# A gather-bound decoder layer: searches lead their rounds by one instead of two, and the Scalar engine's copies go ahead of the pairs' steps

## Chip, cores, metric

One core of one Trainium2 chip runs the whole program. The metric is the device time of one execution in microseconds (us), the median of several; the program is otherwise fixed, with float32 inputs and outputs. Engines are named as in the profile: PE (TensorE; PEld is its weight load), DVE (VectorE), ACT (ScalarE), POOL (GpSimd, which issues the gathers) and SP (SyncE, plain loads and stores).

## The reference

One decoder layer for 1024 prompt rows and 8 sample rows of width 1024. A first part (conditioning, normalisation, one projection into a short convolution and a chunked gating, an output projection) is not touched. The second part is a lookup among 16384 experts, each one row of `expert_u` and one of `expert_v`:

```
def peer_block(xb, w_q, sub_keys, expert_u, expert_v):
    q = (xb @ w_q).reshape(tb, 8, 2, 128)                 # 8 heads
    s = einsum('thpc,hpkc->thpk', q, sub_keys)            # 2 x 128 scores
    sv, si = top_k(s, 16)
    cand = sv[:, :, 0, :, None] + sv[:, :, 1, None, :]
    cv, ci = top_k(cand.reshape(tb, 8, 256), 16)          # 16 of the 256 sums
    expert = si[.., ci // 16] * 128 + si[.., ci % 16]     # 8 x 16 = 128 experts per row
    g = softmax(cv)
    act = gelu(einsum('tkd,td->tk', expert_u[expert], xb))
    return einsum('tk,tkd->td', g * act, expert_v[expert])
```

So every prompt row reads 128 rows of `expert_u` and 128 of `expert_v`, 4 KB each: 2048 gathers of 128 rows, 0.5 MB a gather.

## The kernel before, in words

`peer` holds the second part. Its 8 blocks of 128 rows are done in 32 rounds (`ROUNDS`), four to a block; a round is one pair of heads, 32 experts for each of 128 rows (`WIDE = 32`). Each engine has its own program, written out in order, and the engines meet at semaphores only; an engine never passes a waiting instruction.

Round n on each engine:

- POOL issues 32 gathers of `expert_u` for round n, into a ring of 8 row buffers, and between them 32 gathers of `expert_v` for round n-1, into another ring of 8 (L1093, L1105). Gather g of u waits until DVE has done product g-8, a gather of v until PE has used that slot four tiles at a time (`v_used`). The first u gather of a round waits for the round's indices (`u_idx_ready`).
- DVE does the 32 products of a round (`product`, L1350: u row times x row, summed into `dot`), and between them, at products numbered in `places`, one `search` for each head in `heads_of(n)`. A search (`retrieve`, L1268 to L1321) is the two-stage top 16 and ends in `expert_f`. After the odd head of a pair, `soften` (L1332 to L1338) lowers the sums by their maximum, waits for ACT's exponential and divides by the total. The round ends in `weigh` (L1358).
- PE turns the weights of round n-1 (L1464), turns the pair found in round n-1 (`turn_picked`, L1453), and then does 8 quads of round n-1's v rows (`quad`, L1483). After quads 0, 1 and 2 it puts one head each of `heads_of(n)`: `queries` (L1426), `turn_queries` (L1434, waits for ACT's copy `q_sb`), `scores` (L1442, waits for ACT's copy `qT_sb`).
- ACT does the gelu of the dots (L1193), `keep_weight` (L1202), `keep_picked` (L1183), and then for each head of the round `keep_head`: the copies `q_sb` (L1154), `qT_sb` (L1156), `s_sb` (L1160; this one also waits until the search before has read the old scores). After the odd head of a pair comes `picked`: it waits for the end of that head's search, copies the indices `u_idx` (L1169), loads the table of Exp and takes the exponential (L1171), and loads the table of Gelu again (L1172).

Which heads a round holds sets the lead. Before, heads 0 to 3 are projected ahead of round 0 (0 and 1 are searched ahead of it, 2 and 3 within it), and round n takes heads 2n+4 and 2n+5, so a pair is found two rounds ahead of its gathers. From round 20 on a round takes three heads (`places` 6, 14, 22 instead of 10, 19) until all 72 are done: rounds 20 to 28 have three, round 29 one. Of three heads the odd one is second in rounds 20, 22, 24, 26 and 28, and first and third in the others.

```
            for n in range(ROUNDS + 1):            # ACT
                ...
                if n < ROUNDS:
                    for hd in heads_of(n):
                        keep_head(hd)
                        if hd % 2:
                            picked(hd // 2)
```

Of the kernel before, what the change touches and what calls it, by code (L numbers as in the profile page):

```python
# [9 lines left out]
ALU = mybir.AluOpType  # L10
ACT = mybir.ActivationFunctionType
# [3 lines left out]
P = 128  # L15
# [10 lines left out]
TOPK = 16  # L26
# [849 lines left out]
def peer(nc, t, scratch, ident, w_q, spare, keysT):  # L876
# [12 lines left out]
    KEPT = 8  # L889
    LAST = TILES * (ROUNDS - 1)  # L890
    with ExitStack() as ctx:
        def sb(name, shape, dt=F32):
            return ctx.enter_context(nc.sbuf_tensor(name, shape, dt))

        def sem(name):
            return ctx.enter_context(nc.semaphore(name))
# [26 lines left out]
        best = sb("best", [P, 2, TOPK])  # L923
        gate = [sb(f"gate{i}", [P, 2, TOPK]) for i in range(KEPT + 1)]
# [17 lines left out]
        eps = sb("p_eps", [P, 1])  # L942
        warm = sb("warm", [P, 1])
# [27 lines left out]
        def found_in(n):  # L971

            if n < 0:
                return (0, 1)
            return [hd // 2 for hd in heads_of(n) if hd % 2]

        def heads_of(n):


            first = 2 * n + 4 + max(0, n - 20)  # L980
            return range(min(first, HEADS * (NB + 1)), min(first + (2 if n < 20 else 3), HEADS * (NB + 1)))

        def v_place(g):
# [26 lines left out]
        s_done = sem("s_done")  # L1010
        s_copied = sem("s_copied")
        head_step = sem("head_step")
        soft_step = sem("soft_step")
        exp_done = sem("exp_done")
        picked_turned = sem("picked_turned")
# [114 lines left out]
        def _(act):  # L1130
# [5 lines left out]
            def turn(blk):  # L1136

                for n, ps in enumerate((ps_a, ps_b)):
                    act.wait_ge(h2_turned, 2 * blk + n + 1)
                    nc.scalar.activation(h2T[:, 4 * n:4 * n + 4, :], ps[:, :, :], ACT.Copy).then_inc(h2T_done, 1)  # L1140

            def keep_x(blk):

                act.wait_ge(h2_landed, 16 * blk + 16)
                if blk:
                    act.wait_ge(dots_done, WIDE * 4 * blk)
                nc.scalar.activation(ps_x[:, :], h2_in[:, :], ACT.Copy).then_inc(x_kept, 1)

            def keep_head(hd):

                if hd % HEADS == 0 and hd:
                    turn(hd // HEADS)
                act.wait_ge(q_done, hd + 1)
                nc.scalar.activation(q_sb[:, :], flat_a[:, 0:QCOLS], ACT.Copy).then_inc(q_copied, 1)  # L1154
                act.wait_ge(qT_done, hd + 1)
                nc.scalar.activation(qT_sb[:, :], flat_b[:, 0:QCOLS], ACT.Copy).then_inc(qT_copied, 1)  # L1156
                act.wait_ge(s_done, hd + 1)
                if hd:
                    act.wait_ge(head_step, CHAIN * (hd - 1) + SEARCHED)
                nc.scalar.activation(s_sb[:, :, :].rearrange("p a b -> p (a b)"), flat_a[:, 0:QCOLS], ACT.Copy  # L1160
                                     ).then_inc(s_copied, 1)

            def picked(n):

                if n < ROUNDS:
                    act.wait_ge(head_step, CHAIN * 2 * (n + 1))
                    if n >= KEPT:
                        act.wait_ge(dots_done, WIDE * (n - KEPT + 1))
                    nc.scalar.activation(u_idx[n % KEPT][:, :], expert_f[n % 2][:, 0, :], ACT.Copy).then_inc(u_idx_ready, 1)  # L1169
                act.wait_ge(soft_step, 4 * n + 1)  # L1170
                nc.scalar.activation(gate[n % (KEPT + 1)][:, :, :], gate[n % (KEPT + 1)][:, :, :], ACT.Exp).then_inc(exp_done, 1)  # L1171
                nc.scalar.activation(warm[:, :], eps[:, :], ACT.Gelu)  # L1172

            def keep_picked(n):

# [12 lines left out]
            def gelu(n):  # L1188

                act.wait_ge(dots_done, WIDE * (n + 1))  # L1190
                if n:
                    act.wait_ge(weight_done, n)
                nc.scalar.activation(act_u[:, :], dot[:, n % 2, :], ACT.Gelu).then_inc(gelu_done, 1)  # L1193

            def keep_weight(n):

                act.wait_ge(weight_turned, n + 1)
                if n >= 2:
                    act.wait_ge(v_used, QUADS * (n - 1))
                for a in range(4):  # L1200
                    src = ps_weight[32 * a:32 * a + 32, a:P:4].rearrange("p (j r) -> p j r", j=4)
                    last = nc.scalar.activation(diagonal(spread[n % 2], 4, QUADS, a), src, ACT.Copy)  # L1202
                last.then_inc(spread_done, 1)

            def normalise(ps, b, rows):

                if b:
                    act.wait_ge(out_stored, 16 * b)
                act.wait_ge(y_done, b + 1)
                nc.scalar.activation(out_rows[rows, :], ps[rows, :], ACT.Copy).then_inc(y_kept, 1)  # L1210
                act.wait_ge(y_kept, b + 1)
                nc.scalar.activation(y_junk[rows, :], out_rows[rows, :], ACT.Square, accum_out=y_stat[rows, 0:1]
                                     ).then_inc(y_ssq, 1)
                act.wait_ge(y_ssq, b + 1)
                nc.scalar.activation(y_stat[rows, 1:2], y_stat[rows, 0:1], ACT.Sqrt, scale=1.0 / D, bias=eps[rows, 0:1]
                                     ).then_inc(y_std, 1)

            keep_x(0)
            turn(0)
            for hd in range(4):  # L1220
                keep_head(hd)
                if hd % 2:
                    picked(hd // 2)
            for n in range(ROUNDS + 1):
                if n >= 1:
                    gelu(n - 1)
                if n % 4 == 0 and 4 <= n < ROUNDS:
                    keep_x(n // 4)
                if n % 4 == 1 and n >= 5:
                    normalise(ps_y, n // 4 - 1, slice(0, P))  # L1230
                if n >= 1:
                    keep_weight(n - 1)
                for found in found_in(n - 1):
                    keep_picked(found)
                if n < ROUNDS:
                    for hd in heads_of(n):
                        keep_head(hd)
                        if hd % 2:
                            picked(hd // 2)
            act.wait_ge(sample_dots, NS)  # L1240
            nc.scalar.activation(act_s[:, :, :], dot_s[:, :, :], ACT.Gelu).then_inc(sample_gelu, 1)
            act.wait_ge(sample_weight, 1)
# [7 lines left out]
        def _(dve):  # L1250
# [7 lines left out]
            def retrieve(hd):  # L1258
# [66 lines left out]
                own.settle()  # L1325
                assert own.n == CHAIN, own.n

            def soften(n):

                own = Steps(dve, soft_step, 4 * n)  # L1330
                kept = gate[n % (KEPT + 1)][:, :, :]
                own.did(dve.tensor_tensor(kept, best[:, :, :], best[:, :, 0:1].to_broadcast([P, 2, TOPK]), ALU.subtract))  # L1332
                dve.wait_ge(exp_done, n + 1)
                own.did(dve.tensor_reduce(total[:, :], kept, AX, ALU.add))
                own.settle()
                own.did(dve.reciprocal(inverse[:, :], total[:, :]))
                own.settle()
                own.did(dve.tensor_tensor(kept, kept, inverse[:, :].rearrange("p (h o) -> p h o", o=1).to_broadcast(  # L1338
                    [P, 2, TOPK]), ALU.mult))
                own.settle()  # L1340
                if n >= ROUNDS:
                    dve.wait_ge(picked_turned, n - 1)
                    flat = kept.rearrange("p h k -> p (h k)").rearrange("p (o k) -> p o k", o=1)
                    dve.tensor_copy(gate_four[n % 2][:, :, :], flat.to_broadcast([P, 4, WIDE])).then_inc(gate_four_done, 1)
# [28 lines left out]
            def search(hd):  # L1373

                retrieve(hd)
                if hd % 2:
                    soften(hd // 2)

            search(0)
            search(1)  # L1380
            for n in range(ROUNDS):
                if n % 4 == 0:
                    dve.wait_ge(x_kept, n // 4 + 1)
                heads = list(heads_of(n))
                places = (6, 14, 22) if len(heads) == 3 else (10, 19)[:len(heads)]
                for k in range(WIDE):
                    product(WIDE * n + k, ps_x[:, :], dot[:, n % 2, k:k + 1], dots_done)
                    if n % 4 == 1 and n >= 5 and k == 5:
                        emit(n // 4 - 1, slice(0, P), gate2_b)
                    if n == 0 and k in (3, 9):  # L1390
                        search(2 if k == 3 else 3)
                    if k in places:
                        search(heads[places.index(k)])
                weigh(n)
# [10 lines left out]
        def _(pe):  # L1405
# [101 lines left out]

            pe.wait_ge(const_done, 6)
            turn(0)
            for hd in range(4):  # L1510
                for f, of in head_parts(hd):
                    f(of)
            for n in range(ROUNDS + 1):
# [46 lines left out]
```

## Time and profile before

| | us |
|---|---|
| median of three executions | 3448.59 |
| lowest and highest of them | 3446.67, 3451.38 |
| the profiled execution, its own time | 3449.65 |
| its span in the profile | 3447.9 |
| first gather of round 0 issued | 637.08 |
| busy PE, DVE, ACT, POOL | 1769.8, 1987.8, 383.6, 1960.0 |

Times in the rows are microseconds from the start of the span. The span covers all but some 2 us of the profiled execution's time. The busy share of the DMA engines and the rate in GB/s, taken over a stretch between two gathers, tell whether the gathers kept coming; a row of the timeline gives start, duration, engine, line, what is written and read, and in brackets how long the engine had been idle before and what let it go on.

### The profile page before, as it was taken

The page shows a single profiled execution, that of the slowest core. Times are in us where ns is not written, and L with a number is a line of the kernel's source. Part 1 is how long each engine was busy: PE and PEld are TensorE (multiplying, and loading weights), DVE is VectorE, ACT ScalarE, POOL GpSimd, SP SyncE. Part 2 cuts the span into 40 slices and gives each one's busy share as a digit, 9 for nine tenths or more (in the row PEclk, how much of TensorE's full clock was granted, in tenths as well). Part 3 has the DMA queues.
Part 4 walks back from the last instruction along what each step waited for, and adds up shares of the span by engine and source line. Part 5 has one row for each costly group of instructions (what it writes and reads, how often), then busy time and mean ns, then how long its engine had stood idle before and what let it go on. Part 6 is the DMA issues. An engine that isn't in the chain of part 4 may idle for free.

```text
span 3447.9 us, 25745 instructions
## 1 busy us (share of the span) xinstructions
PE 1769.8 (51%) x7978; PEld 723.2 (21%) x7978; DVE 1987.8 (58%) x5165; ACT 383.6 (11%) x961; POOL 1960.0 (57%) x2091
## 2 busy tenths in 40 slices
PE   4399998434444444444444444444544454443335
PEld 3244443311111111111111111112212222221001
DVE  0121412676667666666666666666767676776442
ACT  0202101100011000100011101000111111111000
POOL 0000000267777776777677767776667676766775
PEclk8699999766666766675666656666766676776556
DMA  9500104489999999999999999998999998999998
GB/s 353 212 0 25 74 0 156 155 339 409 409 409 403 409 404 406 406 408 400 406 407 406 400 407 402 407 404 349 379 365 400 366 410 343 410 373 395 409 409 348
DMA packets 334186, 1169.71 MB, mean 339 GB/s; under 512 B 39222, under 2 KB 46150, under 8 KB 332008
## 3 DMA queue, kind: packets, MB, share of 16 engines
q0 software_dynamic: 298256, 1090.65, 80.0%
q1 hardware_dynamic: 29368, 73.60, 6.0%
q10 hardware_dynamic: 6432, 3.90, 0.4%
q8 instruction: 60, 0.98, 0.1%
q14 instruction: 70, 0.57, 0.0%
HBM read 1154.54 MB, written 13.48 MB: 339 GB/s over the span
## 4 chain that ended last, share of the span: by engine, by line
DMA 31%; POOL 20%; DVE 14%; issue 9%; PE 8%; ACT 1%; POOLq 0%; DVEq 0%; ACTq 0%
DMA v_rows<-in_expert_v_dram,v_idx 14%; POOL v_rows L1105 10%; DMA u_rows<-in_expert_u_dram,u_idx 10%; POOL wide L1093 7%; DMA wide<-in_expert_u_dram,u_idx 6%; PE ps_y L1483 6%; DVE u_rows L1350 3%; POOL u_rows L1093 3%; DVE wide L1350 2%; PE ps_a L1426 1%; DVE pick L1308 1%; DVE pick L1314 1%; DVE pick_f L1319 1%; DVE top_i L1273 1%; DVE top_i L1280 1%
## 5 line engine op out<-in xcount | busy, mean ns | idle before, releaser
L1483 PE MATMUL ps_y<-v_rows,spread 128*32 128x512 f32 x4032 | 844.0, 983 | 1305.2 <-DMA v_rows<-in_expert_v_dram,v_idx 1304.9
L1105 POOL DMA_INDIRECT v_rows<-in_expert_v_dram,v_idx x1008 | 953.0, 945 | 471.1 <-issue 277.6
L1350 DVE CUSTOM_DVE_ANT_0 wide<-wide,ps_x 128x1024 f32<-128x1024 f32 x512 | 615.6, 1219 | 418.4 <-DMA wide<-in_expert_u_dram,u_idx 417.7
L1350 DVE CUSTOM_DVE_ANT_0 u_rows<-u_rows,ps_x 128x1024 f32<-128x1024 f32 x512 | 613.8, 1219 | 388.5 <-DMA u_rows<-in_expert_u_dram,u_idx 386.4
L1093 POOL DMA_INDIRECT wide<-in_expert_u_dram,u_idx x512 | 485.7, 949 | 211.1 <-issue 118.5
L1093 POOL DMA_INDIRECT u_rows<-in_expert_u_dram,u_idx x512 | 483.4, 944 | 174.4 <-issue 102.5
L1483 PEld LDWEIGHTS ps_y<-v_rows,spread 128*32 128x32 f32 x4032 | 164.6, 151 | 1859.1 <-issue 1849.6
L1426 PE MATMUL ps_a<-wide,h2T 128*128 128x256 f32 x1152 | 289.7, 408 | 29.6 <-ACT h2T L1140 27.3
L1426 PEld LDWEIGHTS ps_a<-wide,h2T 128*128 128x128 f32 x1152 | 229.4, 205 | 141.8 <-issue 80.4
L624 POOL DMA_DIRECT2D wide<-in_w_q_dram x1 | 1.1, 1077 | 393.7 <-PE mix_pair L794 393.7
L794 PE MATMUL mix_pair<-hT,wide 128*128 128x512 f32 x512 | 220.8, 593 | 0.0
L794 PEld LDWEIGHTS mix_pair<-hT,wide 128*128 128x128 f32 x512 | 96.9, 190 | 121.0 <-issue 120.5
L868 PE MATMUL mix_pair<-w_out,yT 128*128 128x512 f32 x256 | 110.5, 593 | 0.8 <-DVE yT L762 0.8
L1193 ACT ACTIVATE act_u<-dot 128x32 f32<-128x32 f32 x32 | 7.3, 229 | 829.5 <-DVE dot L1350 829.5
L1169 ACT ACTIVATE u_idx<-expert_f 128x32 uint32<-128x32 f32 x32 | 7.3, 229 | 773.4 <-DVE expert_f L1321 773.4
L1350 DVE DVE_READ_ACCUMULATOR2_ANT dot<- 128x1 f32 x1024 | 84.0, 82 | 0.0
L1434 PE MATMUL ps_b<-ident,q_sb 128*128 128x128 f32 x144 | 33.3, 315 | 98.6 <-ACT q_sb L1154 98.6
L1154 ACT ACTIVATE q_sb<-ps_a 128x256 f32<-128x256 f32 x72 | 27.4, 381 | 496.7 <-PE ps_a L1426 496.7
L1442 PE MATMUL ps_a<-keysT,qT_sb 128*128 128x128 f32 x288 | 55.3, 318 | 34.1 <-ACT qT_sb L1156 34.1
L741 DVE TENSOR_TENSOR z<-rest,mix_pair 128x512 f32<-128x512 f32 x8 | 5.5, 688 | 109.1 <-PE mix_pair L794 109.1
L619 POOL MEMSET ones_row<- 1x128 f32 x1 | 0.2, 194 | 108.3 <-POOLq L89 108.3
L868 PEld LDWEIGHTS mix_pair<-w_out,yT 128*128 128x128 f32 x256 | 48.4, 190 | 61.5 <-issue 59.8
(230 smaller groups left out, 1690.0 us busy)
## 6 DMA issues: line engine op xcount, KB each, us to landing
ada_w<-in_w_ada_dram SPq DMA_DIRECT2D x12, 2048.0 KB, 14.6
v_rows<-in_expert_v_dram,v_idx POOLq DMA_INDIRECT x1008, 8.7
wide<-in_w_in_dram SPq DMA_DIRECT2D x1, 10240.0 KB, 38.0
x_in<-in_x_prompt_dram SPq DMA_DIRECT2D x16, 512.0 KB, 4.3
wide<-in_w_q_dram POOLq DMA_DIRECT2D x1, 8192.0 KB, 23.6
wide<-in_expert_u_dram,u_idx POOLq DMA_INDIRECT x512, 8.9
u_rows<-in_expert_u_dram,u_idx POOLq DMA_INDIRECT x512, 8.8
w_out<-in_w_out_dram SPq DMA_DIRECT2D x1, 4096.0 KB, 45.6
```

What stands on the lines that cost most here:

```text
L794: last = pe.matmul(out, w_in[:, k, col:col + P], hT[:, k, :], start=(k == 0), stop=(k == KD - 1))
L868: last = pe.matmul(ps_o[b % 2][:, n * HALF:(n + 1) * HALF], yT[:, k, b * P:(b + 1) * P], w_out[:, k, n * HALF:(n + 1) * HALF], start=(k == ...
L1093: pool.indirect_dma_start(u_rows[g % RING][:, :], None, t["expert_u"][0], bass.IndirectOffsetOnAxis(ap=idx, axis=0)).then_inc(u_landed[g % ...
L1105: pool.indirect_dma_start(home[:, :], None, t["expert_v"][0], bass.IndirectOffsetOnAxis(ap=idx, axis=0)).then_inc(landed, 16)
L1273: own.did(dve.max_index(top_i[:, p, 0:8], top_v[:, p, 0:8], s_sb[:, p, :]))
L1280: own.did(dve.max_index(top_i[:, p, 8:16], top_v[:, p, 8:16], s_less[:, p, :]))
L1308: own.did(dve.tensor_tensor(pick[:, p, :, :], count[:, :].rearrange("p (o r) -> p o r", o=1).to_broadcast([P, TOPK, TOPK]), pair_f[:, p, : ...
L1314: own.did(dve.tensor_tensor(pick[:, p, :, :], pick[:, p, :, :], top_f[:, p:p + 1, :].to_broadcast([P, TOPK, TOPK]), ALU.mult))
L1350: dve.tensor_tensor_reduce(rows[:, :], rows[:, :], x, 1.0, 0.0, ALU.mult, ALU.add, acc).then_inc(done, 1)
L1426: last = pe.matmul(flat_a[:, 0:QCOLS], h2T[:, k, :], w_q[:, k, h * QCOLS:(h + 1) * QCOLS], start=(k == 0), stop=(k == KD - 1))
L1442: last = pe.matmul(flat_a[:, p * P:(p + 1) * P], qT_sb[:, p * P:(p + 1) * P], keysT[:, 2 * h + p, :], start=True, stop=True)
L1483: last = pe.matmul(ps_y[32 * j:32 * j + 32, c * HALF:(c + 1) * HALF], spread[n % 2][:, 32 * m:32 * m + 32], homes[j][0][:, c * HALF:(c + 1 ...
```

## The change

Three edits, all in `peer`:

1. **Lead.** `heads_of(n)` starts at 2n+2 instead of 2n+4. Only heads 0 and 1 are projected and searched ahead of round 0, and round 0 searches two heads, not four. Rounds 20 to 29 now take three heads each.
2. **ACT's copies first.** A round's `keep_head` calls all come ahead of its `picked` calls; the Gelu table is loaded once a round, between them.
3. **The exponential moves.** `picked` only copies the indices. The lowering (`lower`, a new function with its own semaphore `lowered`) stays behind the search; ACT takes the exponential in the next round right after the gelu (`exponentials`), and DVE divides after product 2 of that round.

```diff
         def found_in(n):
             if n < 0:
-                return (0, 1)
+                return (0,)
             return [hd // 2 for hd in heads_of(n) if hd % 2]
         def heads_of(n):
-            first = 2 * n + 4 + max(0, n - 20)
+            first = 2 * n + 2 + max(0, n - 20)
...
-                act.wait_ge(soft_step, 4 * n + 1)
+
+            def exponentials(n):
+
+                act.wait_ge(lowered, n + 1)
                 nc.scalar.activation(gate[n % (KEPT + 1)][:, :, :], gate[n % (KEPT + 1)][:, :, :], ACT.Exp).then_inc(exp_done, 1)
-                nc.scalar.activation(warm[:, :], eps[:, :], ACT.Gelu)
...
             turn(0)
-            for hd in range(4):
+            for hd in range(2):
                 keep_head(hd)
-                if hd % 2:
-                    picked(hd // 2)
+            picked(0)
             for n in range(ROUNDS + 1):
                 if n >= 1:
                     gelu(n - 1)
+                for found in found_in(n - 1):
+                    exponentials(found)
...
                     for hd in heads_of(n):
                         keep_head(hd)
-                        if hd % 2:
-                            picked(hd // 2)
+                    nc.scalar.activation(warm[:, :], eps[:, :], ACT.Gelu)
+                    for found in found_in(n):
+                        picked(found)
...
+            def lower(n):
+
+                dve.tensor_tensor(gate[n % (KEPT + 1)][:, :, :], best[:, :, :], best[:, :, 0:1].to_broadcast([P, 2, TOPK]),
+                                  ALU.subtract).then_inc(lowered, 1)
+                dve.wait_ge(lowered, n + 1)
+
             def soften(n):
-                own = Steps(dve, soft_step, 4 * n)
+                own = Steps(dve, soft_step, 3 * n)
                 kept = gate[n % (KEPT + 1)][:, :, :]
-                own.did(dve.tensor_tensor(kept, best[:, :, :], best[:, :, 0:1].to_broadcast([P, 2, TOPK]), ALU.subtract))
                 dve.wait_ge(exp_done, n + 1)
...
-                    soften(hd // 2)
+                    lower(hd // 2)
...
-                    if n == 0 and k in (3, 9):
-                        search(2 if k == 3 else 3)
+                    if k == 2:
+                        for found in found_in(n - 1):
+                            soften(found)
...
             turn(0)
-            for hd in range(4):
+            for hd in range(2):
                 for f, of in head_parts(hd):
                     f(of)
```

How the instructions move, at the three places that the prediction speaks of. First ACT in round 20, the first round with three heads (`q_sb`, `qT_sb`, `s_sb` are a head's copies, `u_idx` the indices of a pair, `gate` its exponential, `act_u` the gelu that ends the round). Before:

```order
L1160 ACTIVATE s_sb<-ps_a 128x256
L1154 ACTIVATE q_sb<-ps_a 128x256
L1156 ACTIVATE qT_sb<-ps_b 128x256
L1160 ACTIVATE s_sb<-ps_a 128x256
L1169 ACTIVATE u_idx<-expert_f 128x32
L1171 ACT_TABLE_LOAD
L1171 ACTIVATE gate<-gate 128x32
L1172 ACT_TABLE_LOAD
L1172 ACTIVATE warm<-p_eps 128x1
L1154 ACTIVATE q_sb<-ps_a 128x256
L1156 ACTIVATE qT_sb<-ps_b 128x256
L1160 ACTIVATE s_sb<-ps_a 128x256
```

And in the change, the same stretch to the start of the next round:

```order
L1155 ACTIVATE q_sb<-ps_a 128x256
L1157 ACTIVATE qT_sb<-ps_b 128x256
L1161 ACTIVATE s_sb<-ps_a 128x256
L1155 ACTIVATE q_sb<-ps_a 128x256
L1157 ACTIVATE qT_sb<-ps_b 128x256
L1161 ACTIVATE s_sb<-ps_a 128x256
L1242 ACT_TABLE_LOAD
L1242 ACTIVATE warm<-p_eps 128x1
L1170 ACTIVATE u_idx<-expert_f 128x32
L1196 ACTIVATE act_u<-dot 128x32
L1175 ACT_TABLE_LOAD
L1175 ACTIVATE gate<-gate 128x32
```

The third head's copies stood behind the pair's indices and exponential and now stand ahead of them; the exponential stands behind the gelu.

Second, PE ahead of round 0 and within it. Here `ps_a<-wide,h2T` are a head's queries, `ps_w<-ident,expert_f` is the turn of a pair and `ps_t<-ident,weight` begins round 1. Before, from the second head on:

```order
L1426 MATMUL ps_a<-wide,h2T 128x256 x8
L1434 MATMUL ps_b<-ident,q_sb 128x128 x2
L1442 MATMUL ps_a<-keysT,qT_sb 128x128 x2
L1453 MATMUL ps_w<-ident,expert_f 128x128 x2
L1426 MATMUL ps_a<-wide,h2T 128x256 x8
L1434 MATMUL ps_b<-ident,q_sb 128x128 x2
L1442 MATMUL ps_a<-keysT,qT_sb 128x128 x2
L1426 MATMUL ps_a<-wide,h2T 128x256 x8
L1434 MATMUL ps_b<-ident,q_sb 128x128 x2
L1442 MATMUL ps_a<-keysT,qT_sb 128x128 x2
L1464 MATMUL ps_t<-ident,weight 128x128
```

In the change:

```order
L1437 MATMUL ps_a<-wide,h2T 128x256 x8
L1445 MATMUL ps_b<-ident,q_sb 128x128 x2
L1453 MATMUL ps_a<-keysT,qT_sb 128x128 x2
L1464 MATMUL ps_w<-ident,expert_f 128x128
L1437 MATMUL ps_a<-wide,h2T 128x256 x8
L1445 MATMUL ps_b<-ident,q_sb 128x128 x2
L1453 MATMUL ps_a<-keysT,qT_sb 128x128 x2
L1437 MATMUL ps_a<-wide,h2T 128x256 x8
L1445 MATMUL ps_b<-ident,q_sb 128x128 x2
L1453 MATMUL ps_a<-keysT,qT_sb 128x128 x2
L1475 MATMUL ps_t<-ident,weight 128x128
```

Before, the first of these heads is head 3 and two pairs are turned behind it; now it is head 1, one pair is turned, and the two heads of round 0 are heads 2 and 3.

Third, DVE from the end of a pair's search to the division (`total`, `inverse` and the last `gate` are `soften`, `dot` are products). Before, at the second pair:

```order
L1321 SCALAR_TENSOR_TENSOR expert_f<-pick_f 128x4x16
L1332 TENSOR_TENSOR gate<-best 128x32
L1334 TENSOR_REDUCE total<-gate 128x2
L1336 RECIPROCAL inverse<-total 128x2
L1338 TENSOR_TENSOR gate<-gate,inverse 128x32
L1350 ISA wide,dot<-wide,ps_x 128x1024
```

In the change, behind the third product of round 1:

```order
L1360 ISA wide,dot<-wide,ps_x 128x1024
L1360 ISA dot 128x1
L1344 TENSOR_REDUCE total<-gate 128x2
L1346 RECIPROCAL inverse<-total 128x2
L1348 TENSOR_TENSOR gate<-gate,inverse 128x32
L1360 ISA wide,dot<-wide,ps_x 128x1024
```

The rest of a round's products, its weighing and three products of the next round now stand between the search and the division. POOL's gathers keep their order.

## Rows read from the trace of the kernel before

**Rows 1.** Windows: stretch, length, busy us (count) by engine, PEclk, DMA share, GB/s.

```profile
637.08:717.73 80.65, 19.96 (x74) 14.80 (x74) 62.60 (x210) 15.06 (x34) 30.04 (x32) 0.63 0.55 195
962.68:2302.48 1339.80, 611.16 (x2836) 215.53 (x2832) 887.87 (x2301) 140.59 (x352) 969.69 (x1024) 0.66 1.02 405
2302.48:3113.27 810.79, 385.21 (x1810) 162.92 (x1802) 568.11 (x1646) 104.47 (x267) 544.40 (x576) 0.70 0.96 378
2941.05:3021.80 80.75, 40.15 (x192) 17.43 (x196) 61.69 (x185) 11.18 (x26) 60.71 (x65) 0.75 1.03 409
```

**Rows 2.** Timeline of POOL: first u gathers of rounds 0, 1, 2, 11.

```profile
637.08 1.00 POOL L1093 DMA_INDIRECT wide<-in_expert_u_dram,u_idx  x1 [29.35 <-ACT u_idx L1169]
...
717.73 0.94 POOL L1093 DMA_INDIRECT wide<-in_expert_u_dram,u_idx  x1 [0.41 <-issue]
...
797.82 0.94 POOL L1093 DMA_INDIRECT wide<-in_expert_u_dram,u_idx  x1 [0.30 <-issue]
...
1547.43 0.94 POOL L1093 DMA_INDIRECT wide<-in_expert_u_dram,u_idx  x1 [0.30 <-issue]
```

**Rows 3.** Timeline of DVE, round 0: products (L1350), starts of searches (L1268).

```profile
641.64 1.22 DVE L1350 CUSTOM_DVE_ANT_0 wide<-wide,ps_x 128x1024 f32<-128x1024 f32 x1 [2.66 <-DMA wide<-in_expert_u_dram,u_idx]
...
646.95 1.22 DVE L1350 CUSTOM_DVE_ANT_0 wide<-wide,ps_x 128x1024 f32<-128x1024 f32 x1 [0.21 <-DMA wide<-in_expert_u_dram,u_idx]
...
648.10 0.48 DVE L1268 MAX8 top_v<-s_sb 128x8 f32<-128x128 f32 x2
...
656.01 1.22 DVE L1350 CUSTOM_DVE_ANT_0 u_rows<-u_rows,ps_x 128x1024 f32<-128x1024 f32 x1
...
657.16 1.22 DVE L1350 CUSTOM_DVE_ANT_0 u_rows<-u_rows,ps_x 128x1024 f32<-128x1024 f32 x1
...
682.61 0.49 DVE L1268 MAX8 top_v<-s_sb 128x8 f32<-128x128 f32 x2 [8.16 <-ACT s_sb L1160]
```

**Rows 4.** Timeline of PE, round 20: the third head.

```profile
2348.51 4.58 PE L1426 MATMUL ps_a<-wide,h2T 128*128 128x256 f32 x16
...
2364.85 0.69 PE L1434 MATMUL ps_b<-ident,q_sb 128*128 128x128 f32 x2 [11.76 <-ACT q_sb L1154]
```

**Rows 5.** Timeline of ACT, round 20: indices to third head.

```profile
2361.24 0.23 ACT L1169 ACTIVATE u_idx<-expert_f 128x32 uint32<-128x32 f32 x1 [18.45 <-DVE expert_f L1321]
2361.49 1.28 ACT L1171 ACT_TABLE_LOAD   x1
2362.78 0.23 ACT L1171 ACTIVATE gate<-gate 128x32 f32<-128x32 f32 x1
2363.03 1.28 ACT L1172 ACT_TABLE_LOAD   x1
...
2364.43 0.37 ACT L1154 ACTIVATE q_sb<-ps_a 128x256 f32<-128x256 f32 x1
```

**Rows 6.** Timeline of POOL, round 20: two gathers in a row.

```profile
2357.57 0.94 POOL L1093 DMA_INDIRECT u_rows<-in_expert_u_dram,u_idx  x1 [0.30 <-issue]
2372.50 0.94 POOL L1105 DMA_INDIRECT v_rows<-in_expert_v_dram,v_idx  x1 [14.00 <-issue]
```

**Rows 7.** Waits: engine, line, releaser; us in total, times, longest.

```profile
PE ps_b L1434 <- ACT q_sb L1154: 98.6, 72, 12.7
```

**Rows 8.** Timeline of ACT: index copies of rounds 1 and 10.

```profile
781.84 0.23 ACT L1169 ACTIVATE u_idx<-expert_f 128x32 uint32<-128x32 f32 x1 [29.41 <-DVE expert_f L1321]
...
1532.64 0.23 ACT L1169 ACTIVATE u_idx<-expert_f 128x32 uint32<-128x32 f32 x1 [28.96 <-DVE expert_f L1321]
```

**Rows 9.** Timeline of ACT at the start of round 20.

```profile
2310.14 0.23 ACT L1193 ACTIVATE act_u<-dot 128x32 f32<-128x32 f32 x1 [20.41 <-DVE dot L1350]
2310.27 1.01 ACT L1147 ACTIVATE ps_x<-h_in 128x1024 f32<-128x1024 f32 x1
2314.33 0.91 ACT L1202 ACTIVATE spread<-ps_t 32x32 f32<-32x32 f32 x4 [3.04 <-PE ps_t L1464]
```

**Rows 10.** Source line L1171: waits for the exponential; us, times.

```profile
  DVE total L1334: 52.7, 36
```

More of the change, by code:

```diff
@@ L1012, in peer @@
         head_step = sem("head_step")
+        lowered = sem("lowered")
         soft_step = sem("soft_step")
```

## The prediction

> **What bounds the kernel now.** I read the windows first, cut at the first u gather of a round, because the gathers move nearly all the bytes. The reader should see three stretches there [rows 1]. Rounds 4 to 19 hold 1024 gathers in 1339.80 us, 1.31 us each, at 405 GB/s with the DMA engines' share at 1.02: the gathers bound them, and nothing an engine does faster shows. DVE is busy 887.87 / 16 = 55.5 us of each round's 83.7, so it has 28 us to spare. Round 0, with only u gathers, takes 80.65 us at 195 GB/s and share 0.55. Rounds 20 to 28 run at 378 GB/s and 0.96. So the time that an order of engine work can give back lies in round 0 and in rounds 20 to 28, and I read those two with the timelines.
>
> Round 0 is paced by DVE. POOL's first gather is issued at 637.08 and round 1's first at 717.73 [rows 2]; between them a gather waits for the product eight before it. DVE's products follow each other at 657.16 - 656.01 = 1.15 us, and a search from its first instruction to the next product takes 656.01 - 648.10 = 7.91 us [rows 3]. Four searches stand in this round, and the third begins only after 8.16 us of waiting for ACT's copy of the scores [rows 3].
>
> Rounds 20 to 28 hold three heads. In round 20 PE ends the third head's queries at 2348.51 + 4.58 = 2353.09 and stands until 2364.85 for the copy `q_sb`, 11.76 us [rows 4]. ACT is not late with work: it waited 18.45 us for the second head's search, which ended at 2361.24, and then did indices, two table loads and the exponential before the copy at 2364.43 [rows 5]. PE's quads stand behind that wait, and they free the v ring; POOL's next v gather starts after 14.00 us, at 2372.50 [rows 6]. The waits list has this wait as 98.6 us in all with a longest of 12.7 [rows 7], a stall of several rounds. The row names "issue" as POOL's releaser, so that the quads released it is my reading.
>
> **The change, part by part.**
>
> *The lead, round 0.* The start stays: heads 0 and 1 are still searched first, so the first gather stays at 637.08. Then I count DVE to product 24, since gather 32, round 1's first, needs it. Product 3 starts at 646.95 as before [rows 3], plus 0.6 us for the division, whose three small instructions I estimate from the exponential's 0.23 [rows 5]. Rows then land no faster than a gather takes, 1.28 us as an estimate from 0.524 MB at 409 GB/s [rows 1], so product 10 starts near 656.5 and ends near 657.7. Search of head 2: 7.9, to 665.6. Nine products (11 to 19) at 1.15: 675.9. Search of head 3: 7.9, and 0.2 for the lowering, to 684.0. Five products: 5.7, to 689.7. Its indices are copied near 684.3, earlier than needed. Round 1 then starts near 690 in place of 717.73: **28 us**. The two removed searches are 15.8 of it, the 8.16 wait goes because the scores of heads 2 and 3 are copied before product 10, and the rest is two divisions with their waits. Ends: 20 if a new wait for scores or rows of 8 us comes in, 31 if product 10 is reached 3 us sooner.
>
> *The lead, later.* The index copy of a round now serves the next round, not the one after. In round 1 it was made at 781.84 and round 2's first gather went at 797.82, 16.0 us of slack; over the 19 two-head rounds 1 to 19 the least is round 10's, 1532.64 to 1547.43, 14.8 us [rows 2, 8]. ACT now does only one table load between the copies and `picked`, which waits for the search anyway. Cost: 0. With three heads the second search stands after product 14, not 19, so the slack grows.
>
> *ACT's copies first, rounds 20 to 28.* The third head's copies no longer stand behind `picked`. ACT's `s_sb` copies still wait until the search before has read the old scores, a wait on its first six steps and not on its end. PE's queries of the third head need the second's `s_sb`, so the first search; that one starts after product 6 and PE arrives after v row 11. I take the stall as gone. The bytes of the stretch are 810.79 us at 378 GB/s; at rounds 4 to 19's 405 they take 756.7, **54 us** less, and at round 27's 409, which also holds three heads, 749.3, or 61 less [rows 1]. I take 52, leaving 2 for waits of the first search for its scores. The low end, 27, is a stall half left. Round 29 now also has three heads; DVE's 28 us of slack against 7.9 for each added search covers it.
>
> *The exponential.* It leaves DVE's path: 36 waits, 52.7 us in all [rows 10]. I count nothing, as DVE has its slack; without that cover it would be a further 52.7. On ACT the table load (1.28) and exponential (0.23), 1.54 us as they lie from 2361.49 to 2363.03 [rows 5], now stand ahead of `keep_x` and of the weights' copy. There ACT waited 3.04 us for PE's turn after `keep_x` [rows 9], so the weights' copy is not later. `keep_x` is, by 1.54 us in the 7 later blocks, and DVE starts those rounds that much later: at most 11 us, and 0 with 28 us to spare. The lowering and the table loads that fall away (one Exp and one Gelu each round remain) are off the path. The four sample pairs' gates reach PE only after product 2 of a round: at most three products at 2 x 1.31 us, 7.9, in three rounds, under the 8 x 1.31 = 10.5 us that the v ring holds. Cost 0, and 3 x 7.9 = 24 without that cover.
>
> The Trainium skill's page "ScalarE: Activation LUTs", section "What ACT_TABLE_LOAD costs", puts a switch of tables at about 2.66 us, a load of 1283 ns and a drain of 1380. By that the moved exponential would be 2.9 us and `keep_x` up to 7 x 2.9 = 20 us later in all, an estimate, and the sum up to 20 less. The trace agrees on the load and shows no drain: the exponential starts 1.29 us after the load does [rows 5].
>
> *SP and POOL.* A block's turn comes one round later, behind the same load; the eight small loads of the sample rows wait for the last head, which moves from first to third in round 29, two rounds ahead of their use: 0. POOL's order is unchanged.
>
> **The sum.** 3449.65 (the profiled execution) - 28 - 52 = 3369.65. That execution is 1.06 above the median of 3448.59, so I predict 3369.
>
> **The rivals.**
>
> 1. *The PE stall moves or was misread.* The third head still waits, now for the second's `s_sb`, or POOL was held by something else. For: ACT is in order and still waits on searches; the releaser in [rows 6] is not PE. Against: 14.00 us begin while PE stands for 11.76. Then only round 0 gains: 3449.65 - 28 - 1 = 3421.
> 2. *Round 0 gives nothing.* A wait for the scores of heads 2 and 3, projected later now, eats it. For: 8.16 us of such a wait exist. Against: their queries can run from 637 on, and need to be done by 657. Then 3449.65 - 52 - 1 = 3397.
> 3. *The lead is too short, slower.* POOL reaches a round's first u gather before the indices. It decides from 14.8 us of lateness against the rows of before; each us beyond costs 19 rounds 1 us. Being late by a landing time, 641.64 - 637.08 = 4.56 us [rows 2, 3], is 19 x 4.56 = 87 lost against 80 gained: 3456. For: the lead falls by a round, 83.7 us, to 16 us. Against: nothing new stands between the search's end and the copy.
> 4. *The gathers take back all of it*, because the queue and not its feeding is slow in the weak stretches: 3449. Against: the share of 0.55 in round 0. The Trainium skill, "Perfetto Trace Analysis", section "What "DMA-bound" means", names larger descriptors as what matters for a kernel bound on DMA engines. The trace agrees for rounds 4 to 19 only.
>
> **How the numbers follow.** A run of this kernel can tell about 0.2%, 7 us, from no change. Forecast 0.75, of which 0.04 lies below its own range of 3357 (31 and 61 gained) to 3398 (24 and 27); rival 1 0.09, rival 2 0.07, rival 3 0.05, rival 4 0.04. The range for 8 in 10 takes in rival 2 and the forecast's ends, 3356 to 3403, and leaves out rivals 1, 3 and 4 and the tail below, 0.22, about what is allowed. Faster: 0.75 + 0.09 + 0.07 = 0.91; same 0.04; slower 0.05.
>
> **What would show it.** Round 1's first gather near 690; rounds 20 to 28 near 757 us together at some 405 GB/s; `ps_b` waits for `q_sb` no longer above a few us; no wait of POOL for `u_idx` but the first; no DVE wait before `total`, now 52.7 / 36 = 1.46 us each. It is wrong if POOL waits for indices at round starts, or if rounds 20 to 29 still fall under 400 GB/s.

## The result, and the profile after

The change takes 3370.55 us (median of four, 3370.1 to 3371.35) against 3448.98 (3446.67 to 3451.38) for the kernel before, a ratio of 0.9773 with a 95% interval of 0.9756 to 0.979. The prediction was 3369.

The windows of the changed kernel, cut as in [rows 1] at the first u gathers of round 0, rounds 4 to 19 and rounds 20 to 28 (stretch, length, busy us and count of PE, PEld, DVE, ACT and POOL, PE clock, DMA share, GB/s):

```profile
633.32:687.28 53.96, 11.06 (x44) 8.21 (x43) 46.31 (x129) 5.91 (x15) 30.05 (x32) 0.63 0.79 289
933.91:2271.44 1337.53, 606.26 (x2836) 214.76 (x2832) 888.51 (x2300) 140.82 (x352) 967.99 (x1024) 0.66 1.02 406
2271.44:3029.61 758.17, 382.23 (x1801) 159.20 (x1797) 567.36 (x1642) 93.74 (x252) 545.75 (x577) 0.70 1.02 405
```

Read the last two columns against [rows 1]. Round 0 goes from 80.65 to 53.96 us and from 195 to 289 GB/s. Rounds 4 to 19 stay, 1339.80 and 1337.53 us at a share of 1.02. Rounds 20 to 28 go from 810.79 to 758.17 us and from 378 to 405 GB/s, the rate of the stretch ahead of them. The stretches outside these add the rest of the 79.5 us by which the span is shorter: 3.8 us lie ahead of the first gather, 637.08 before and 633.32 here (over the profiles of the kernels below that share this part it lies between 633.3 and 638.1, so this is no gain), and rounds 29 to the end are 4.2 us longer, 2.8 of them in round 29. 26.7 + 52.6 + 3.8 + 0.6 (rounds 1 to 19) - 4.2 = 79.5.

The timeline of POOL, first u gathers of rounds 0, 1 and 2, which answer to [rows 2]:

```profile
633.32 1.00 POOL L1094 DMA_INDIRECT wide<-in_expert_u_dram,u_idx  x1 [29.45 <-ACT u_idx L1170]
...
687.28 0.94 POOL L1094 DMA_INDIRECT wide<-in_expert_u_dram,u_idx  x1 [0.42 <-issue]
...
767.25 0.94 POOL L1094 DMA_INDIRECT wide<-in_expert_u_dram,u_idx  x1 [0.30 <-issue]
```

The timeline of DVE in round 0, which answers to [rows 3]: products 0, 11 and 24 (L1360) and the starts of the two searches (L1273):

```profile
637.72 1.22 DVE L1360 CUSTOM_DVE_ANT_0 wide<-wide,ps_x 128x1024 f32<-128x1024 f32 x1 [4.72 <-DMA wide<-in_expert_u_dram,u_idx]
...
654.38 0.48 DVE L1273 MAX8 top_v<-s_sb 128x8 f32<-128x128 f32 x2
...
662.29 1.22 DVE L1360 CUSTOM_DVE_ANT_0 wide<-wide,ps_x 128x1024 f32<-128x1024 f32 x1
...
672.57 0.48 DVE L1273 MAX8 top_v<-s_sb 128x8 f32<-128x128 f32 x2
...
685.28 1.22 DVE L1360 CUSTOM_DVE_ANT_0 wide<-wide,ps_x 128x1024 f32<-128x1024 f32 x1
```

Both searches begin the moment the product before them ends (no idle time stands in brackets), where the third of four stood for 8.16 us.

PE and ACT in round 20, at the third head, answer to [rows 4] and [rows 5]. PE's timeline first, then ACT's:

```profile
2316.86 4.88 PE L1437 MATMUL ps_a<-wide,h2T 128*128 128x256 f32 x16
...
2322.22 0.44 PE L1445 MATMUL ps_b<-ident,q_sb 128*128 128x128 f32 x2 [0.47 <-ACT q_sb L1155]
```

```profile
2321.78 0.39 ACT L1155 ACTIVATE q_sb<-ps_a 128x256 f32<-128x256 f32 x1 [9.33 <-PE ps_a L1437]
...
2323.88 0.38 ACT L1161 ACTIVATE s_sb<-ps_a 128x256 f32<-128x256 f32 x1 [0.80 <-DVE top_v L1282]
...
2324.28 1.28 ACT L1242 ACT_TABLE_LOAD   x1
...
2330.02 0.23 ACT L1170 ACTIVATE u_idx<-expert_f 128x32 uint32<-128x32 f32 x1 [4.24 <-DVE expert_f L1326]
```

PE waits 0.47 us for the copy, not 11.76. ACT's third `s_sb` (2323.88) waited for the sixth step of a search, the last that reads the old scores (L1278; the row names L1282, which begins right behind it), and not for the search's end; that end comes just ahead of 2330.02, where the indices are copied. In the waits list the pair of [rows 7] falls from 98.6 to 34.2 us with a longest of 0.5:

```profile
PE ps_b L1445 <- ACT q_sb L1155: 34.2, 72, 0.5
```

### The profile page after: what moved, and what is told of

The parts are those of the page before. It is cut to its first block, busy times and chain, and to the rows that moved or that the text cites. A ratio compares the mean times of both kernels' runs of the same rounds, so it can differ in the third digit from the quotient of the medians.

```text
span 3368.4 us, 25767 instructions
## 1 busy us (share of the span) xinstructions
PE 1756.1 (52%) x7978; PEld 716.8 (21%) x7978; DVE 1990.1 (59%) x5165; ACT 370.3 (11%) x947; POOL 1959.8 (58%) x2091
## 4 chain that ended last, share of the span: by engine, by line
DMA 36%; POOL 16%; DVE 15%; issue 8%; PE 7%; ACT 0%; POOLq 0%; DVEq 0%; ACTq 0%
DMA v_rows<-in_expert_v_dram,v_idx 16%; DMA wide<-in_expert_u_dram,u_idx 11%; DMA u_rows<-in_expert_u_dram,u_idx 9%; POOL v_rows L1106 8%; PE ps_y L1494 6%; POOL wide L1094 6%; DVE u_rows L1360 4%; POOL u_rows L1094 2%; DVE wide L1360 2%; DVE pick L1313 1%; DVE pick L1319 1%; DVE pick_f L1324 1%; PE ps_a L1437 1%; DVE top_i L1278 1%; DVE top_i L1285 1%
## 5 line engine op out<-in xcount | busy, mean ns | idle before, releaser
L1360 DVE CUSTOM_DVE_ANT_0 wide<-wide,ps_x 128x1024 f32<-128x1024 f32 x512 | 617.2, 1220 | 419.2 <-DMA wide<-in_expert_u_dram,u_idx 402.7
L1360 DVE CUSTOM_DVE_ANT_0 u_rows<-u_rows,ps_x 128x1024 f32<-128x1024 f32 x512 | 614.7, 1219 | 370.4 <-DMA u_rows<-in_expert_u_dram,u_idx 367.9
L1437 PEld LDWEIGHTS ps_a<-wide,h2T 128*128 128x128 f32 x1152 | 227.7, 204 | 119.4 <-issue 79.4
L1360 DVE DVE_READ_ACCUMULATOR2_ANT dot<- 128x1 f32 x1024 | 84.3, 82 | 0.0
L315 PE MATMUL ps_ada<-ada_w,cT 128*32 128x128 f32 x768 | 39.3, 390 | 38.4 <-DMA ada_w<-in_w_ada_dram 38.4
## 6 DMA issues: line engine op xcount, KB each, us to landing
w_out<-in_w_out_dram SPq DMA_DIRECT2D x1, 4096.0 KB, 44.1
```

The source lines that it names most:

```text
L315: last = pe.matmul(ps_ada[r][Q * j:Q * j + Q, :], cT[:, k, :], ada_w[r][:, k, j * P:(j + 1) * P], start=(k == 0), stop=(k == KD - 1))
L1360: dve.tensor_tensor_reduce(rows[:, :], rows[:, :], x, 1.0, 0.0, ALU.mult, ALU.add, acc).then_inc(done, 1)
L1437: last = pe.matmul(flat_a[:, 0:QCOLS], h2T[:, k, :], w_q[:, k, h * QCOLS:(h + 1) * QCOLS], start=(k == 0), stop=(k == KD - 1))
```

## Experiments

Times are medians; ratios are to the kernel before, measured on the same chip.

**Copies first, lead of two.** The change without its first edit:

```diff
-            first = 2 * n + 2 + max(0, n - 20)
+            first = 2 * n + 4 + max(0, n - 20)
...
-            for hd in range(2):
-                keep_head(hd)
-            picked(0)
+            keep_head(0)
+            keep_head(1)
+            picked(0)
+            exponentials(0)
+            keep_head(2)
+            keep_head(3)
+            picked(1)
```

(and heads 2 and 3 searched after products 3 and 9 of round 0, as before; pair 1 is divided in round 1).

> The change without its first edit: a lead of two rounds as before, but ACT's copies ahead of the indices and the exponential in the next round. My theory (two separate gains): rounds 20 to 28 lose their stall, 758 us together as in the change, not 811; round 0 keeps its four searches and most of the wait of 8 us for scores, but two divisions with their waits (2 x 2.4 us) and 3 us of table loads leave it, some 73 us, not 54. Time 3449 - 52 - 8 = 3389 (3382 to 3400). Rival (the shorter lead is what frees rounds 20 to 28, since heads and turns shift by a round): those rounds stay near 811 and the time is 3437 or more.

3394.68 us, ratio 0.9837 (0.9821 to 0.9854). Windows of round 0 and of rounds 20 to 28:

```profile
634.51:711.56 77.05, 21.72 (x74) 16.05 (x74) 61.46 (x204) 9.08 (x26) 30.06 (x33) 0.61 0.58 204
2296.25:3054.37 758.12, 383.05 (x1804) 158.12 (x1802) 567.87 (x1644) 93.83 (x255) 545.81 (x576) 0.70 1.02 404
```

Rounds 20 to 28 have all of their gain without the shorter lead: 758.12 us. Round 0 was expected near 73 and is 77.05. The wait of DVE for scores did not shrink with the table loads, 8.45 us for 8.16:

```profile
678.66 0.49 DVE L1282 MAX8 top_v<-s_sb 128x8 f32<-128x128 f32 x2 [8.45 <-ACT s_sb L1165]
```

PE projects head 4 only after it has turned pair 1, for which head 3's search must have ended, so the wait begins with that search's end and the table loads were not in its way. PE's row of the projection (the search's last step starts at 668.49):

```profile
670.04 6.06 PE L1448 MATMUL ps_a<-wide,h2T 128*128 128x256 f32 x16
```

**Lead of one, alone.** The kernel before with the other prologue and no other edit:

```diff
-            first = 2 * n + 4 + max(0, n - 20)
+            first = 2 * n + 2 + max(0, n - 20)
...
-            for hd in range(4):
+            for hd in range(2):
                 keep_head(hd)
                 if hd % 2:
                     picked(hd // 2)
```

> The kernel before with the lead of one round and nothing else: picked and the exponential stay behind the odd head's copies. My theory: round 0 falls from 80.7 us to some 56 (one division with its wait stays in it), rounds 20 to 28 stay near 811, round 29 now holds three heads and loses a few us more: 3449 - 24 + 3 = 3428 (3420 to 3440). Rival (the lead frees the late rounds too): 3371 to 3380. Second rival (round 0 needs the copies first as well): round 0 stays above 70 us, 3445.

3426.93 us, ratio 0.993 (0.9913 to 0.9946). The same two windows:

```profile
637.34:692.57 55.23, 10.96 (x44) 8.16 (x43) 46.98 (x132) 8.91 (x19) 30.39 (x33) 0.62 0.77 284
2276.30:3089.51 813.21, 380.60 (x1807) 162.10 (x1801) 567.78 (x1645) 104.77 (x264) 545.39 (x577) 0.69 0.96 377
```

Round 0 has its gain, 55.23 us, and rounds 20 to 28 have none, 813.21. With the run above the two gains are separate: 3451.09 - 3394.68 = 56.4 and 3451.09 - 3426.93 = 24.2 us, together 80.6, where the whole change gave 3448.98 - 3370.55 = 78.4. This run also keeps DVE's wait for the exponential, 52.7 us in 36 times as before, which is worth nothing in the rounds that the gathers bound: rounds 1 to 19 take 2276.30 - 692.57 = 1583.73 us with it and 2271.44 - 687.28 = 1584.16 in the change.

**Indices in line again.** The change with one edit half undone:

```diff
                     for hd in heads_of(n):
                         keep_head(hd)
+                        if hd % 2:
+                            picked(hd // 2)
                     nc.scalar.activation(warm[:, :], eps[:, :], ACT.Gelu)
-                    for found in found_in(n):
-                        picked(found)
```

> The change with one part undone: the indices are copied (and so the end of the search is waited for) directly behind the odd head's copies again, the exponential and its table loads stay in the next round. My theory: what PE stood for was ACT's wait for the search, so the third head's copy is late again by 11.8 less the 3.2 us of table loads and exponential, and rounds 20 to 28 lose some 30 of the 52.6 us gained: 3401 (3390 to 3415), with waits of PE at the turn of the queries of 6 to 9 us. Rival (the table loads and the exponential between the copies made the stall): 3371 to 3376.

3398.1 us, ratio 0.9845 (0.9828 to 0.9861). Windows of round 0 and of rounds 20 to 28, then PE's third head and ACT's two rows at that time in round 20:

```profile
637.58:691.05 53.47, 10.95 (x44) 8.14 (x43) 46.40 (x129) 5.90 (x15) 30.05 (x33) 0.63 0.80 292
2275.36:3063.14 787.78, 387.05 (x1803) 160.41 (x1801) 567.85 (x1642) 93.28 (x252) 544.76 (x577) 0.69 0.98 388
```

```profile
2334.50 0.69 PE L1445 MATMUL ps_b<-ident,q_sb 128*128 128x128 f32 x2 [10.45 <-ACT q_sb L1155]
```

```profile
2333.94 0.23 ACT L1170 ACTIVATE u_idx<-expert_f 128x32 uint32<-128x32 f32 x1 [17.60 <-DVE expert_f L1326]
...
2334.08 0.37 ACT L1155 ACTIVATE q_sb<-ps_a 128x256 f32<-128x256 f32 x1
```

787.78 us: 29.6 of the 52.6 are lost again, by the wait (the copy of the indices behind it takes 0.23 us). ACT stood 17.60 us for the search's end and began the third head's copy 0.14 us after that of the indices; PE stood 10.45, above the 6 to 9 expected.

The other 23 us, and what the shorter lead cost, are shown by this run beside the one before. "Lead of one, alone" has the same heads in the same rounds, and its indices are in line too; it differs in the third edit, the moved exponential with its table loads and the division, and loads the Gelu table for each pair and not once a round. Rounds 20 to 28 take 813.21 us there and 787.78 here. So from the kernel before it is 810.79, 813.21 with the shorter lead, 787.78 with the exponential out of ACT's way as well, and 758.17 with the wait for the search's end behind the copies.

PE's waits for ACT in rounds 20 to 28 alone, first in the kernel before, then in this run, then in the change (us in total, times, longest):

```profile
PE ps_b L1434 <- ACT q_sb L1154: 68.4, 27, 12.7
PE ps_a L1426 <- ACT h2T L1140: 23.0, 3, 15.0
```

```profile
PE ps_b L1445 <- ACT q_sb L1155: 46.9, 27, 11.2
PE ps_a L1437 <- ACT h2T L1141: 17.0, 3, 12.1
```

```profile
PE ps_b L1445 <- ACT q_sb L1155: 12.8, 27, 0.5
PE ps_a L1437 <- ACT h2T L1141: 2.2, 3, 0.7
```

The second line of each pair is a stand that [rows 7] does not hold: `h2T`, ACT's copy of a new block's turned rows, stood behind the same `picked`. Together the stands are 91.4, 63.9 and 15.0 us, so over the change 76.4 and 48.9 for 52.6 and 29.6 us of time: each us for which PE stands costs some 0.6 to 0.7 us.

**A late second search.** The change with the second search of rounds 1 to 19 after product 29, so that a round's indices come late. It prices the lead:

```diff
-                places = (6, 14, 22) if len(heads) == 3 else (10, 19)[:len(heads)]
+                places = (6, 14, 22) if len(heads) == 3 else (10, 29 if n else 19)[:len(heads)]
```

> The change with the second search of rounds 1 to 19 after product 29, not 19, so that a round's indices come some 25 us later, 10 us after POOL wants them. It prices the lead that the change gives up. My theory: POOL stands for the indices at 19 round starts; the part of it that the transfers under way don't hide is worked out from POOL's pace: 58 gathers at 1.28, a landing near 5, a product, a search of 7.9 and the copy make a period near 89 us, not 82.7: 19 x 6 = 114 us, 3485 (3430 to 3560). Rival (the transfers under way hide it): within 10 us of the change, 3371 to 3381.

3527.76 us, ratio 1.0222 (1.0205 to 1.0239). POOL at a round's start, and the window of rounds 1 to 19:

```profile
1057.34 0.94 POOL L1094 DMA_INDIRECT wide<-in_expert_u_dram,u_idx  x1 [11.53 <-ACT u_idx L1170]
...
1058.58 0.93 POOL L1106 DMA_INDIRECT v_rows<-in_expert_v_dram,v_idx  x1 [0.30 <-issue]
```

```profile
690.39:2435.66 1745.27, 730.90 (x3359) 259.32 (x3364) 1063.23 (x2740) 162.04 (x414) 1145.91 (x1216) 0.65 0.94 369
```

POOL waits for the indices at each of the 19 starts, 11.0 to 11.8 us, and rounds 1 to 19 grow from 1584.16 to 1745.27, by 8.5 us a round, not 6. The mechanism was the expected one, the size was not: I had counted a landing of 5 us, and the u gathers of this run land a median of 8.7 us after their issue. The size agrees with POOL's own work plus its wait: 64 gathers, each 0.94 us and 0.30 to the next, 1.24 x 64 = 79.4 us, plus 11.2 makes 90.6, and most rounds take 90.6 to 91.5.

**The second search after product 24.** The same line with 24 in place of 29.

> The change with the second search of rounds 1 to 19 after product 24, not 19: five products at 2.56 us later, so the 15.0 to 16.1 us of slack that the index copies have in the profile of the change shrink to some 2.4 us. My theory (a late index costs only what POOL stands for it, and what is left of the slack is free): within 4 us of the change, 3367 to 3375, rounds 1 to 19 at 1584 us together, no wait of POOL for the indices but the first. Rival (the transfers under way need the whole slack, and every us of it that goes costs part of a us): rounds 1 to 19 grow by 19 x 1 us or more, 3390 or more.

3369.84 us, ratio 0.9768 (0.9753 to 0.9783). ACT's copy of round 1's search and POOL's first gather of round 2, then rounds 1 to 19:

```profile
769.84 0.23 ACT L1170 ACTIVATE u_idx<-expert_f 128x32 uint32<-128x32 f32 x1 [40.23 <-DVE expert_f L1326]
```

```profile
772.49 0.93 POOL L1094 DMA_INDIRECT wide<-in_expert_u_dram,u_idx  x1 [0.30 <-issue]
```

```profile
692.46:2276.52 1584.06, 724.55 (x3344) 257.61 (x3348) 1054.83 (x2732) 163.91 (x414) 1147.11 (x1217) 0.66 1.02 406
```

2.65 us of slack (2.3 to 2.7 in all 19 rounds), and no cost: 1584.06 us. With the run before, the edge lies between the two: 2.3 us early costs nothing, 11 us late costs 8.5. No run lies between them.

**The first half of the indices early.** A step beyond the change, from the finding that round 0 is what is left: the first 16 indices of pair 0 go to POOL when head 0's search ends.

```diff
+            def half_picked(n):
+                act.wait_ge(head_step, CHAIN * (2 * n + 1))
+                nc.scalar.activation(u_idx[n][:, 0:TOPK], expert_f[n][:, 0, 0:TOPK], ACT.Copy).then_inc(half_ready, 1)
...
+            half_picked(0)
             picked(0)
```

(POOL waits for `half_ready` ahead of gather 0 and for `u_idx_ready` ahead of gather 16; `picked(0)` copies the other half.)

> A step beyond the change: the first 16 indices of pair 0 are copied when head 0's search ends, so round 0's first 16 gathers start while head 1 is searched. My theory: the first gather goes 7.9 us earlier, near 625; products still begin when head 1's search ends, near 633, but the ring of 8 rows is full by then, so they need not wait for a landing of 4.6 us and run at 1.15 us each, not 1.3, from the start. Round 1's first gather comes 5 to 7 us sooner: 3364 (3361 to 3368). Rival (round 0 is paced by the two searches and the landing of later rows, so a full ring at its start is used up by product 10 and gives nothing): 3369 to 3372.

3363.44 us, ratio 0.9749 (0.9736 to 0.9762), 7.1 us under the change, the upper end of what was expected. First u gathers of rounds 0 and 1:

```profile
628.04 1.00 POOL L1095 DMA_INDIRECT wide<-in_expert_u_dram,u_idx  x1 [21.45 <-ACT u_idx L1179]
...
681.80 0.93 POOL L1095 DMA_INDIRECT wide<-in_expert_u_dram,u_idx  x1 [0.42 <-issue]
```

Round 0 is not shorter, 53.77 us from gather to gather; it begins sooner, ahead of the end of head 1's search. DVE's products 0 and 24:

```profile
635.70 1.22 DVE L1370 CUSTOM_DVE_ANT_0 wide<-wide,ps_x 128x1024 f32<-128x1024 f32 x1
...
679.81 1.22 DVE L1370 CUSTOM_DVE_ANT_0 wide<-wide,ps_x 128x1024 f32<-128x1024 f32 x1
```

Product 0 starts without a wait, where in the change it stood 4.72 us for its row, and product 24 follows 44.1 us later, for 685.28 - 637.72 = 47.6 in the change. That is the mechanism that was expected. The first gather was expected near 625 and went at 628.04; the part ahead of round 0 differs by some us from profile to profile, so the single starts can't be compared more closely than that.

**Both halves early.** The same for pair 1, and the search of head 3 behind product 31 of round 0 instead of 19.

> The same, and pair 1's first 16 indices are copied when head 2's search ends, with the search of head 3 moved from product 19 to behind product 31 of round 0. My theory: that search leaves DVE's way to product 24, which releases round 1's first gather, so that comes 7.9 us sooner again, and the 16 gathers that then may go cover the search: 3357 (3353 to 3363), round 0 near 46 us from round 1's view. Rival (the later search delays the weights of round 0, PE's quads come late, the v ring of 8 is full and POOL stands, which gives the gain back in round 1): round 1 grows from 80 to 85 us or more, and the time is that of the kernel with pair 0 alone or above it.

3354.07 us, ratio 0.9725 (0.9712 to 0.9738), the fastest version here and 16.5 us under the change. Windows of rounds 0 and 1, then DVE at the old and the new place of the second search:

```profile
629.08:675.50 46.42, 11.60 (x45) 8.75 (x45) 45.87 (x128) 6.37 (x16) 30.13 (x32) 0.66 0.87 323
675.50:756.50 81.00, 31.77 (x156) 12.47 (x160) 65.23 (x187) 7.37 (x21) 60.61 (x65) 0.67 1.03 409
```

```profile
667.01 1.22 DVE L1372 CUSTOM_DVE_ANT_0 wide<-wide,ps_x 128x1024 f32<-128x1024 f32 x1
...
682.05 0.48 DVE L1285 MAX8 top_v<-s_sb 128x8 f32<-128x128 f32 x2
```

At 667.01 a product stands where the search stood, and product 24 begins 43.6 us behind the first gather, for 679.81 - 628.04 = 51.8 in the run with pair 0 alone:

```profile
672.72 1.22 DVE L1372 CUSTOM_DVE_ANT_0 wide<-wide,ps_x 128x1024 f32<-128x1024 f32 x1
```

Round 0 is 46.42 us at 323 GB/s. Round 1 takes 81.00 us at a share of 1.03, against 79.97 in the change and 80.60 with pair 0 alone, so the 85 us or more of the rival with its late quads did not come.

## Why the prediction was right, point by point

- **Round 0 (28 us; 26.7 measured).** The count from the first gather held at every step: product 10 was to end 20.6 us behind it and ended 21.1 behind (654.38), product 19 at 38.8 and 39.3 (672.57), round 1 at 53 and 53.96. The run with the shorter lead alone shows that this edit by itself gives 25.4 of it.
- **Rounds 20 to 28 (52 us; 52.6 measured).** They took the rate of rounds 4 to 19, 405 GB/s, as the term assumed. That PE stood for ACT's wait for the end of a search is shown by putting that wait back, with nothing else: 29.6 us return. The table loads and the exponential behind that wait are the rest, 25.4 us between the two runs with a lead of one. The prediction read the 98.6 us of [rows 7] as this stall; 68.4 of them lie in rounds 20 to 28, and the 23.0 us for `h2T` were left out. My reading that the quads (L1483) held POOL, although [rows 6] names "issue", is borne out by the same gap in rounds 22, 24, 26 and 28 of the kernel before, where POOL stands 10.4 to 16.3 us and the rows name the quads. In round 22, PE's and POOL's:

```profile
2546.76 0.69 PE L1434 MATMUL ps_b<-ident,q_sb 128*128 128x128 f32 x2 [12.72 <-ACT q_sb L1154]
...
2552.57 0.94 POOL L1105 DMA_INDIRECT v_rows<-in_expert_v_dram,v_idx  x1 [12.10 <-PE ps_y L1483]
```

- **The copies come first only because the exponential moved.** The program shows it, no run does: with the exponential still behind the copies, DVE's division behind an odd first head would wait for ACT, and ACT's third `s_sb` for DVE's next search, each for the other.
- **The lead (0).** The copy for round 2 lies at 752.04, POOL's first gather of it at 767.25: 15.2 us, where [rows 2, 8] gave 16.0 for round 1's and 14.8 as the least.

```profile
752.04 0.23 ACT L1170 ACTIVATE u_idx<-expert_f 128x32 uint32<-128x32 f32 x1 [27.44 <-DVE expert_f L1326]
```

  The rival's threshold, lateness beyond the slack, is where the cost began, between 2.3 us early and 11 us late; its price of 1 us per us late was too high, 8.5 for 11.2, since POOL, at 1.24 us a gather, makes good some of it against the 1.31 of a round that the transfers bound.
- **The exponential (0).** It sits where it was put, and the weights' copy is not later: from gelu to spread 2314.33 - 2310.14 = 4.19 us in [rows 9] and 2283.32 - 2279.10 = 4.22 here. ACT's wait for PE gave the cover, 3.04 down to 1.53 us:

```profile
2279.10 0.23 ACT L1196 ACTIVATE act_u<-dot 128x32 f32<-128x32 f32 x1 [22.51 <-DVE dot L1360]
...
2279.35 1.28 ACT L1175 ACT_TABLE_LOAD   x1
...
2280.64 0.23 ACT L1175 ACTIVATE gate<-gate 128x32 f32<-128x32 f32 x1
...
2280.78 1.01 ACT L1148 ACTIVATE ps_x<-h_in 128x1024 f32<-128x1024 f32 x1
...
2283.32 0.91 ACT L1205 ACTIVATE spread<-ps_t 32x32 f32<-32x32 f32 x4 [1.53 <-PE ps_t L1475]
```

  The load takes 1.28 us and the exponential starts 1.29 after it, again without the 1380 ns of drain that the Trainium skill adds in "ScalarE: Activation LUTs", section "What ACT_TABLE_LOAD costs". By the Trainium skill's 2.66 us the cover would, as an estimate, have been nearly used up; the trace decides for 1.29.
- **The rivals.** That the stall moves (3421) is out with PE's waits of 0.5 us, and that a new wait for scores eats round 0 (3397) with its two searches that begin without a wait. That the gathers take all of it back (3449) is out too: with the same bytes in the same sizes the rate over rounds 20 to 28 went from 378 to 405 GB/s. The Trainium skill's "Perfetto Trace Analysis", section "What "DMA-bound" means", has large descriptors as what matters for a kernel bound on its DMA engines. The whole of this kernel is not so bound, by the same two rates; rounds 4 to 19 are, at a share of 1.02, but no run here changed a size.
- **The signs.** POOL waits for `u_idx` at the first gather alone, and no wait stands ahead of `total` (L1344), for 52.7 us before.
- **What the prediction left out.** Round 29 was put at 0 for its two added heads; it grew from 86.98 to 89.76 us, at 389 GB/s. The added heads do not explain it: in "Copies first, lead of two" round 29 holds one head, as before, and takes 3143.98 - 3054.37 = 89.61 us. The cause stays open. The start of the gathers moved by 3.8 us for no reason in the change. These two nearly cancel, and so do the errors of the two large terms (1.3 and 0.6 us), so that the sum came within 2 us is in part luck. The forecast's own lower end counts 24 us for round 0 where its working says 20; with 20 it is 3402, still inside the stated range.

## What to carry to other kernels

Cut the profile into rounds before asking what bounds a kernel: a share of busy DMA that is full in most rounds says nothing of the few where the ring behind the queue runs dry. On an engine that works strictly in order, put the work that others stand for ahead of every wait whose result is needed only later; here one wait, with 3.2 us of copying, table loads and exponential behind it, stood ahead of a 0.4 us copy and held PE 12 us and the gathers 14. A lead of one round is enough when the result comes before the issuer reaches it: measure that slack in the rows. Here nothing was lost with 2.3 us of it, and with indices 11.2 us late three quarters of that were lost.

## What was not expected of the hardware

POOL issues a gather every 1.24 us, and a gather takes 1.28 us at the 409 GB/s of the fastest rounds, an estimate from its 0.524 MB, and 1.31 us over rounds 4 to 19 before. So POOL is only some 3 to 5% from being the bound itself. A round takes it 79.4 us, where rounds 1 to 19 of the change take 83.4 on average, so a late round can win back some 4 us at most. It won back 2.7 of 11.2, which made the late search dearer than expected.
